# The last norm's sums of squares: TensorE with tokens on partitions in place of additions on VectorE

## What is computed

```
f = peer_ffn(h, w_q, sub_keys, u_tab, v_tab)
x = x + gt2[:, None, :] * rms_norm(f, g_post2)

def rms_norm(x, g):
    y = xf * lax.rsqrt(jnp.mean(xf * xf, axis=-1, keepdims=True) + EPS)
    return y * g
```

## Time and profile before

| | |
|---|---|
| runs without a profile (3) | 1819.3 us median, 1819.21 to 1819.33 |
| profiled execution | 1824.03 us, span 1821.9 us |
| TensorE busy | 1750.4 us, 96% of the span |
| VectorE busy | 1094.9 us, 60% |
| GpSimd busy | 1053.3 us, 58% |
| ScalarE busy | 590.6 us, 32% |
| mean granted clock of TensorE | 0.985 |

### The profile page before, as it was taken

The page is one execution under the profiler, slowest core; times in us unless marked ns, Lnnn a source line. Parts: engine busy times, 40 slices in busy tenths (PEclk is TensorE's granted clock), DMA queues, the critical chain, the costliest instruction groups (busy, mean ns, idle before and its releaser), DMA issues.

```text
span 1821.9 us, 31250 instructions
## 1 busy us (share of the span) xinstructions
PE 1750.4 (96%) x12752; PEld 1708.9 (94%) x12752; DVE 1094.9 (60%) x2185; ACT 590.6 (32%) x760; POOL 1053.3 (58%) x693
## 2 busy tenths in 40 slices
PE   5899999999999999999999999999999999999996
PEld 4799988969899999999999999999999999999995
DVE  3732578176577645757662222224688889888884
ACT  5313154343233332323222222222333333333332
POOL 0241010002787788888888888873677777767621
PEclk9899999999999999999999999999999999999998
DMA  7333369575256666575757666667899999999971
GB/s 271 133 150 117 140 247 349 184 257 171 36 117 137 139 134 141 110 151 100 148 113 156 145 140 140 138 136 259 336 358 371 388 358 373 354 374 370 385 285 47
DMA packets 191926, 385.18 MB, mean 211 GB/s; under 512 B 74328, under 2 KB 132056, under 8 KB 176808
## 3 DMA queue, kind: packets, MB, share of 16 engines
q1 hardware_dynamic: 111432, 306.56, 49.5%
q0 software_dynamic: 80352, 76.65, 19.3%
HBM read 318.44 MB, written 64.19 MB: 210 GB/s over the span
## 4 chain that ended last, share of the span: by engine, by line
PE 61%; DVE 7%; issue 4%; ACT 0%; DMA 0%; SPq 0%; DVEq 0%; ACTq 0%
PE ps L1496 31%; PE ps L1516 29%; DVE ul L1686 2%; DVE topi L134 0%; DVE topi L124 0%; DMA ahead_dram<-a 0%; PE ps L1473 0%; DVE top L128 0%; ACT uh L1553 0%; DVE qp L1803 0%; DVE h L1826 0%; DVE h L227 0%; DVE h L222 0%; DVE h L213 0%; DVE pick L217 0%
## 5 line engine op out<-in xcount | busy, mean ns | idle before, releaser
L99 POOL DMA_INDIRECT gates_dram<-gate,where x384 | 652.8, 1700 | 285.1 <-DVE where L250 142.6
L1496 PE MATMUL ps<-hl,uh 128*128 128x260 f32 x2048 | 415.2, 284 | 8.5 <-DVE ul L1686 8.5
L1496 PE MATMUL ps<-hh,ul 128*128 128x260 f32 x2048 | 414.9, 284 | 0.0
L1496 PE MATMUL ps<-hh,uh 128*128 128x260 f32 x2048 | 414.0, 284 | 0.0
L1686 DVE TENSOR_TENSOR ul<-us,uh 128x1024 fp32r<-128x1024 f32 x132 | 161.2, 1224 | 366.8 <-issue 290.9
L1516 PE MATMUL ps<-cl,uh 128*128 128x384 f32 (+1 forms) x1024 | 345.6, 337 | 3.0 <-issue 3.0
L1516 PE MATMUL ps<-ch,ul 128*128 128x384 f32 x1024 | 344.6, 337 | 0.0
L1516 PE MATMUL ps<-ch,uh 128*128 128x384 f32 x1024 | 344.6, 337 | 0.0
L1496 PEld LDWEIGHTS ps<-hl,uh 128*128 128x128 f32 x2048 | 318.1, 190 | 9.7 <-DVE ul L1686 9.5
L1496 PEld LDWEIGHTS ps<-hh,ul 128*128 128x128 f32 x2048 | 317.9, 190 | 0.0
L1496 PEld LDWEIGHTS ps<-hh,uh 128*128 128x128 f32 x2048 | 316.8, 189 | 0.0
(11 more groups left out here) (218 smaller groups left out, 2260.9 us busy)
## 6 DMA issues: line engine op xcount, KB each, us to landing
us<-utab SPq DMA_DIRECT2D x128, 512.0 KB
pairs<-vtab SPq DMA_DIRECT2D x62, 1024.0 KB
wr<-w_ada SPq DMA_DIRECT2D x24, 1024.0 KB, 6.1
gates_dram<-blank SPq DMA_DIRECT2D x24, 1024.0 KB, 9.5
ahead_dram<-a SPq DMA_DIRECT2D x128, 192.0 KB
qp<-ahead_dram SPq DMA_DIRECT2D x32, 768.0 KB
gt<-gates_dram SPq DMA_DIRECT2D x32, 768.0 KB
wr<-w_in SPq DMA_DIRECT2D x14, 1024.0 KB, 4.8
```

The lines of the kernel that those rows point to most:

```text
L99: nc.gpsimd.indirect_dma_start(out=io["gates"].rearrange("g p c a t -> (g p c a t)").unsqueeze(1), out_offset=bass.IndirectOffsetOnAxis(ap ...
L1496: last = nc.tensor.matmul(out[:, half, :], w, r[:, k, half * TH:(half + 1) * TH], start=(k == 0 and q == 0), stop=(k == KD - 1 and q == 2))
```

## The change

The seven additions of squares on VectorE go. TensorE sums each tile's squares by itself: for each k four one-column matmuls, each into a column of its own in bank 0 (columns 64 to 95, ordered by group c and tile k), 32 in all. VectorE then reduces the eight partial sums of each token, and makes the mean. The eight transposes of the samples move to bank 1, and stand between the sums of k = 0 to 3 and those of k = 4 to 7. VectorE copies banks 0 to 3 and ScalarE banks 4 to 7; ScalarE takes the root ahead of k = 5.

```
+        ON_VECTOR = 4
+        sums_of_tokens = ps[0:TD, 0, KD * NS:KD * NS + (SEQ // TD) * KD].rearrange("p (c k) -> p c k", k=KD)
+        turned_samples = ps[:, 1, 0:KD * NS]
...
 TensorE
+                def token_sums(k):
+                    pe.wait_ge(fsq_ok, k + 1)
+                    for c in range(SEQ // TD):
+                        last = nc.tensor.matmul(sums_of_tokens[:, c, k:k + 1], squares[:, k, c * TD:(c + 1) * TD],
+                                                ones[:, 0:1], start=True, stop=True)
+                    if k == KD - 1:
+                        last.then_inc(fss_mm, 1)
                 pe.wait_ge(fn_ok, 1)
-                pe.wait_ge(f_ok, 1)
-                pe.wait_ge(fsq_ok, 1)
+                pe.wait_ge(f_ok, 2)
+                for k in range(KD // 2):
+                    token_sums(k)
                 for k in range(KD):
-                    last = nc.tensor.transpose(ps[:, 0, k * NS:(k + 1) * NS], ...
+                    last = nc.tensor.transpose(turned_samples[:, k * NS:(k + 1) * NS], ...
                 last.then_inc(ft_mm, 1)
-                pe.wait_ge(sum_ok, 1)
-                pe.wait_ge(f_ok, 2)
-                for c in range(SEQ // TD):
-                    last = nc.tensor.matmul(ps[0:TD, 1, c:c + 1], squares[:, 0, c * TD:(c + 1) * TD], ones[:, 0:1],
-                                            start=True, stop=True)
-                last.then_inc(fss_mm, 1)
+                for k in range(KD // 2, KD):
+                    token_sums(k)
+                pe.wait_ge(fs_ok, 1)
                 pe.wait_ge(fr_ok, 1)
...
 ScalarE
-                for k in range(2, KD):
-                    if k == KD - 2:
+                for k in range(ON_VECTOR, KD):
+                    if k == ON_VECTOR + 1:
...
 VectorE
-                for k in range(2):
+                for k in range(ON_VECTOR):
...
-                for k in range(1, KD):
-                    dve.wait_ge(fsq_ok, k + 1)
-                    last = nc.vector.tensor_tensor(squares[:, 0, 0:SEQ], squares[:, 0, 0:SEQ], squares[:, k, 0:SEQ],
-                                                   ALU.add)
-                    if k < KD - 1:
-                        await_step(step(last))
-                last.then_inc(sum_ok, 1)
...
                 dve.wait_ge(fss_mm, 1)
-                nc.vector.tensor_scalar(dr[:], ps[0:TD, 1, 0:SEQ // TD], 1.0 / D, EPS, ALU.mult, ALU.add)\
-                    .then_inc(fms_ok, 1)
+                await_step(step(nc.vector.tensor_reduce(dr[:], sums_of_tokens, AX.X, ALU.add)))
+                nc.vector.tensor_scalar(dr[:], dr[:], 1.0 / D, EPS, ALU.mult, ALU.add).then_inc(fms_ok, 1)
```

More of the change, by code:

```diff
@@ L1347, in peer_stage @@
         fsq_ok = sem("fsq_ok")
-        sum_ok = sem("sum_ok")
         ft_mm = sem("ft_mm")
@@ L1525, in _ @@
                         gathered_sums(2)
+                def token_sums(k):
[5 more added lines that the diff above has]
+                        last.then_inc(fss_mm, 1)
                 pe.wait_ge(fn_ok, 1)
-                pe.wait_ge(f_ok, 1)
-                pe.wait_ge(fsq_ok, 1)
+                pe.wait_ge(f_ok, 2)
+                for k in range(KD // 2):
+                    token_sums(k)
                 for k in range(KD):
-                    last = nc.tensor.transpose(ps[:, 0, k * NS:(k + 1) * NS], sample_rows[:, k * P:(k + 1) * P],
-                                               ident[0:NS, 0:NS])
+                    last = nc.tensor.transpose(turned_samples[:, k * NS:(k + 1) * NS],
+                                               sample_rows[:, k * P:(k + 1) * P], ident[0:NS, 0:NS])
                 last.then_inc(ft_mm, 1)
-                pe.wait_ge(sum_ok, 1)
-                pe.wait_ge(f_ok, 2)
-                for c in range(SEQ // TD):
-                    last = nc.tensor.matmul(ps[0:TD, 1, c:c + 1], squares[:, 0, c * TD:(c + 1) * TD], ones[:, 0:1],
-                                            start=True, stop=True)
-                last.then_inc(fss_mm, 1)
+                for k in range(KD // 2, KD):
+                    token_sums(k)
+                pe.wait_ge(fs_ok, 1)
                 pe.wait_ge(fr_ok, 1)
@@ L1617, in _ @@
                         .then_inc(fm_ok, 1)
-                act.wait_ge(fm_ok, KD - 2)
+                act.wait_ge(fm_ok, KD - ON_VECTOR)
             @block.gpsimd
@@ L1800, in _ @@
                         .then_inc(f_ok, 1)
-                for k in range(1, KD):
-                    dve.wait_ge(fsq_ok, k + 1)
-                    last = nc.vector.tensor_tensor(squares[:, 0, 0:SEQ], squares[:, 0, 0:SEQ], squares[:, k, 0:SEQ],
-                                                   ALU.add)
-                    if k < KD - 1:
-                        await_step(step(last))
-                last.then_inc(sum_ok, 1)
                 dve.wait_ge(ft_mm, 1)
-                nc.vector.tensor_tensor(tsm[:], ps[:, 0, 0:KD * NS].rearrange("p (k t) -> p k t", k=KD),
+                nc.vector.tensor_tensor(tsm[:], turned_samples.rearrange("p (k t) -> p k t", k=KD),
                                         co[:, 3, :, 1:1 + NS], ALU.mult).then_inc(fs_ok, 1)
                 dve.wait_ge(fss_mm, 1)
-                nc.vector.tensor_scalar(dr[:], ps[0:TD, 1, 0:SEQ // TD], 1.0 / D, EPS, ALU.mult, ALU.add)\
-                    .then_inc(fms_ok, 1)
+                await_step(step(nc.vector.tensor_reduce(dr[:], sums_of_tokens, AX.X, ALU.add)))
+                nc.vector.tensor_scalar(dr[:], dr[:], 1.0 / D, EPS, ALU.mult, ALU.add).then_inc(fms_ok, 1)
                 dve.wait_ge(frt_ok, 1)
@@ L1820, in scaled @@
                 def scaled(k):
-                    if k < 2:
+                    if k < ON_VECTOR:
                         dve.wait_ge(f_ok, k + 1)
                     else:
-                        dve.wait_ge(fm_ok, k - 1)
+                        dve.wait_ge(fm_ok, k - ON_VECTOR + 1)
                     nc.vector.tensor_tensor(acc[:, k, 0:SEQ], acc[:, k, 0:SEQ], ps[:, 1, :], ALU.mult).then_inc(t_ok, 1)
```

## The result

The changed kernel takes 1827.2 us (median of 22 runs, 1823.4 to 1839.7), the kernel before 1819.5 in the same sessions (22 runs, 1817.1 to 1824.9). The ratio is 1.0042, with a 95% interval of 1.0032 to 1.0051: 7.6 us slower, between 5.8 and 9.3. The forecast was 1825.5, +6.2 us, in a range of 1821.2 to 1828.0.

The account below looks back on a forecast made before the run. The end's chain ran through VectorE's additions; after the change TensorE's stream of one-column records was to bind, its clock falling. 6.0 (sums) + 0.2 (reduction) + 0 (copies) = +6.2 us on the 1819.3 median: 1825.5, range 1821.2 to 1828.0.

Parts of the forecast that it names:

- What goes, and what is late next: End of kernel: seven VectorE additions, 5.04 us, go; TensorE's own stream, not a wait for squares, is late next.
- Price and count of the records: TensorE's sums: 64 records replace eight, 0.11 us each at full clock; that alone makes the sums 3.1 us late.
- the hole: TensorE's idle time of 2.86 us before the sums, waiting for VectorE's additions; the change fills it with TensorE work.
- The clock: TensorE's granted clock falls to 0.50 during the one-column sums, though its queue is full; chance 0.63.
- The slow spacing: One-column sum records at clock 0.50 follow each other at 0.213 us; 28 of them take 5.96 us.
- Where the clock falls: Fall in the second half of the sums, at 1804.48 as before, 28 records left; sums 6.0 us late.
- an early fall: Clock falling at 1801.4, 51 records and the transposes at half speed; sums 8.9 us late, +9.1 in all, 1828.4.
- The steps after it: After the sums: VectorE's new reduction adds 0.2 us; mean, root, reciprocal as before; broadcast 2.09 us at low clock.
- Copies: VectorE four copies instead of two, ScalarE four instead of six: hidden, value 0; at most 1.8 us without cover.
- Rival 1: Clock stays up through sums and broadcast: +2.3 us, 1821.6, bounds 1.9 to 3.3; chance 0.28.
- Rival 2: One-column sum records run closer, at the transposes' 0.066 us: -0.5 us, 1818.8; chance 0.05.
- Rival 3: ScalarE's copies behind the root bind the scalings: +1 us at the most, on top of others; no chance of its own.

Follow-up runs that it names:

- copies2: The changed kernel with copies shared as before (VectorE two, ScalarE six, root ahead of k = 6); ratio 1.0033 to the kernel before.
- wide128: The changed kernel with each of the 64 sum records streaming 128 columns of ones instead of one; ratio 1.0011 to the kernel before.
- wide32: The changed kernel with each sum record streaming 32 columns of ones instead of one; ratio 1.0029 to the kernel before.
- onepass: The changed kernel with squares rounded to fp32r and two columns of ones, 32 one-pass records instead of 64; ratio 1.0008 to the kernel before.
- hybrid: The kernel before, but VectorE adds only squares k = 1 to 5; TensorE sums k = 6, 7, then the added ones; ratio 0.9990.
- hybrid128: The kernel before with VectorE adding squares k = 1 to 5, TensorE summing k = 6, 7 and the added ones, 128 columns per record; ratio 0.9997.
- best: Against the kernel before: VectorE adds squares k = 1, 2; TensorE sums k = 3 to 7 and the added ones, one fp32r pass, 256 columns, transposes last; ratio 0.9974.
- onepass128: The changed kernel with squares rounded to fp32r, 32 one-pass sum records, 128 columns of ones each; ratio 1.0000 to the kernel before.
- onepass256: The changed kernel with squares rounded to fp32r, 32 one-pass sum records, 256 columns of ones each; ratio 0.9994 to the kernel before.

## Why the prediction held, step by step

- *What goes, and what is late next.* Right. TensorE stands idle no more, it does not wait for squares, and it is TensorE's stream that VectorE waits for, 6.69 us.
- *Price and count of the records.* Right: 64 records, and 0.11 each at full clock. 32 of them take 3.56 us in copies2 (1794.89 to the first transpose at 1798.45). With the clock held up, wide128 takes 8.1 us from the first record to the reduction (1795.13 to 1803.25) where I had 7.7. The kernel before took 4.6, so 3.5 of the 7.7 us of loss are there even at full clock: more work than the hole and the replaced records had room for.
- *The clock.* The choice was right. It was a choice: no row of the kernel before had a stream of such records alone. wide128 shows the reason as far as it can be shown: same count, weights and waits, only the streamed columns changed, and the clock stayed. The other cases (with one, two and 32 columns it fell in the sums; with 128 in a single pass behind them; with 128 in two passes and 256 in one it held through the broadcast) go the same way, each in one profiled execution. "TensorE: Matmul & The Clock Gate" in the Trainium skill, Part 1, asks only for no idle gaps; in the sums of the changed kernel, wide32, copies2 and onepass TensorE had none and the clock fell all the same, so the measurement decides against that reading. The sentence of its Part 4, that transposes do not count as busy in the same way, points the right way for one-column matmuls too; of transposes alone no run here shows it.
- *The slow spacing.* 0.213 forecast; the second block of the changed kernel, all of it at 0.50, gives (6.99 - 0.3) / 31 = 0.216. Right.
- *Where the clock falls.* This is the term that was mis-sized. The forecast took over the place of the fall from the kernel before, 4.5 us behind the first record, where TensorE had stood idle first; no row showed where it falls in a full stream. With it the sums were to be 6.0 us late. In the profile of the changed kernel it fell at 2.95 us, and the sums take 12.04 us against 4.61 before (1799.97 to 1804.58): 7.4 late. In copies2 it fell at 4.35 us, and the sums take 11.00, 6.4 late. So 1.0 us of the miss is the place of the fall. The other 0.4 is small change, seen in copies2: 0.04 in the first block, 0.09 in the transposes (0.59 us from the first of them to the next sum, where I had 0.5), and the rest in the second block, where the clock fell 0.15 us sooner than forecast and the spacing was a little wider. The forecast named an early fall (up to +9.1), and the spread of falls seen, 2.7 to 4.9 us into the stage over these runs, lies within it. That the total came as near as +7.6 to +6.2 hung on where the clock happened to fall, which the forecast could not place.
- *The steps after it.* From the reduction to the broadcast it is 0.99 us, where mean to broadcast took 0.67 (1804.58 to 1805.25): 0.3 more, where I had 0.2. The reduction and its gap take 0.22. The other 0.10 stands between the reciprocal and the broadcast, 0.33 us from start to start where it was 0.23. It is there in all runs with the new wait on fs_ok ahead of the broadcast and not in hybrid, hybrid128 and best, which have none there; that the wait is the cause is not shown otherwise. The broadcast takes 2.05, unchanged. Copies: 0, by copies2. The rest of the stage: 14.61 against 14.54.
- *Rivals.* Rival 1 (the clock stays) was priced at +2.3 us. wide128 is that case made real: its stage is 2.89 us longer than before and its time +2.0 (-0.7 to 4.7). By the stage, the change would not have paid had the clock stayed. Rival 2 (closer records) is refuted by every run, down to one pass: no spacing of sum records under 0.11. Rival 3 (copies) by copies2.

What stays open: why the fall comes at 2.7 us in one execution and at 4.9 in another. The changed kernel and copies2 give TensorE the same stream, and it fell at 2.95 us in one and at 4.35 in the other. No kernel was profiled often enough to say how far the place moves by itself.

## What to carry to other kernels

A matmul with one column is not free: here each of its records cost 0.11 us, the spacing of the weight loads. So moving a sum to TensorE is to be priced by records times that spacing, also where TensorE stands idle: the hole held 2.9 us and the sums needed 7. A stream of such records did not keep the clock up although the engine was never idle; with 128 columns in each fp32 record, which cost almost no time (3.66 us for 32 records against 3.56), it stayed up. Where an engine waits, give it the part of the work that fits into the wait (here two or five of eight tiles), not all of it.

## What the runs showed of the hardware

- TensorE's clock fell from 2.4 to 1.2 GHz while the engine was busy for 2.90 of 2.90 us, with one-column matmuls. With 128 columns in each fp32 record it stayed, for the same number of records, each still about 0.11 us (0.111 with one column in copies2, 0.114 with 128 in wide128).
- The records of an fp32r matmul (one pass) follow each other at 0.111 us (onepass), as those of one pass of an fp32 matmul do (0.111, copies2), so the rounded form costs half in such a stream.
- Up to 256 columns of fp32r under one weight load cost little: the first 16 records take 1.77 us from start to the next group with 2 columns, 1.83 with 128 and 1.98 with 256 (onepass, onepass128, onepass256).
